# A two-layer float32 transformer kernel on one core: the first transfers regrouped, and four transposes moved behind a projection half

## What is computed

```python
q_a, c_kv, q_idx, k_idx, w_idx, q_b, k_b, v_b = jnp.split(x @ w_in, cuts, axis=-1)
o_a = dsa_attention(q_a, rms_norm(c_kv, kv_norm), q_idx, k_idx, w_idx * IDX_HEADS ** -0.5, w_uk, w_uv)
o_b = stick_breaking_attention(q_b, k_b, v_b)
return concatenate([o_a, o_b]) @ w_out
```

## Time and profile before

| | us |
|---|---|
| median of 3 runs | 619.95 |
| lowest, highest | 619.73, 620.75 |
| the profiled execution | 620.58 |
| its span in the profile | 618.8 |

### The profile page before, as it was taken

The page is one execution under the profiler, slowest core; times in us unless marked ns, Lnnn a source line. Parts: engine busy times, 40 slices in busy tenths (PEclk is TensorE's granted clock), DMA queues, the critical chain, the costliest instruction groups (busy, mean ns, idle before and its releaser), DMA issues.

```text
span 618.8 us, 10403 instructions
## 1 busy us (share of the span) xinstructions
PE 604.3 (98%) x3729; PEld 527.6 (85%) x3729; DVE 413.0 (67%) x668; ACT 340.0 (55%) x631; POOL 25.6 (4%) x49
## 2 busy tenths in 40 slices
PE   7999999999999999999999999999999999999995
PEld 6988887798888888888889998978988888888884
DVE  4698746677756655665887666767776566665546
ACT  5776667266644554455566665653655545555430
POOL 0101012020000000000020000002000000000000
PEclk9999999999999999999999999999999999999999
DMA  7877434447755565555446454362776655555401
GB/s 269 269 222 257 137 103 150 157 135 237 236 174 187 188 203 193 180 184 190 138 145 231 135 164 144 130 211 68 247 235 199 204 201 177 183 187 198 139 1 68
DMA packets 31202, 109.48 MB, mean 177 GB/s; under 512 B 3440, under 2 KB 4464, under 8 KB 31040
## 3 DMA queue, kind: packets, MB, share of 16 engines
q1 hardware_dynamic: 29600, 102.77, 50.2%
q0 software_dynamic: 1568, 6.23, 3.1%
HBM read 107.94 MB, written 1.05 MB: 176 GB/s over the span
## 4 chain that ended last, share of the span: by engine, by line
PE 90%; DMA 3%; DVE 2%; ACT 2%; SPq 1%; POOL 1%; issue 1%; DVEq 0%
PE bank L947 27%; PE bank L879 24%; PE bank L925 13%; PE bank L882 12%; PE bank L893 5%; DMA raw<-stream_in 3%; PE bank L872 2%; PE bank L996 2%; PE bank L1007 1%; PE bank L987 1%; DVE wlo L592 1%; ACT whi L321 1%; POOL hTs L313 1%; PE bank L1194 1%; PE bank L1102 1%
## 5 line engine op out<-in xcount | busy, mean ns | idle before, releaser
L592 DVE TENSOR_TENSOR wlo<-raw,whi 128x1024 fp32r<-128x1024 f32 x190 | 226.6, 1222 | 69.7 <-ACT whi L321 69.5
L321 ACT CAST whi<-raw 128x1024 fp32r<-128x1024 f32 x190 | 192.7, 1049 | 21.1 <-DMA raw<-stream_in 20.8
L879 PE MATMUL bank<-hTs,whi 128*128 128x512 f32 x640 | 160.1, 392 | 0.0
L879 PEld LDWEIGHTS bank<-hTs,whi 128*128 128x128 f32 x640 | 116.1, 189 | 21.4
L947 PE MATMUL bank<-whi,oThi 128*128 128x512 f32 x240 | 94.9, 395 | 0.0
L947 PE MATMUL bank<-whi,oTlo 128*128 128x512 f32 x240 | 93.7, 390 | 0.0
L947 PE MATMUL bank<-wlo,oThi 128*128 128x512 f32 x240 | 93.5, 390 | 0.0
L882 PEld LDWEIGHTS bank<-hTs,wlo 128*128 128x128 f32 x640 | 87.3, 190 | 6.2
L882 PE MATMUL bank<-hTs,wlo 128*128 128x256 f32 x640 | 89.2, 282 | 0.0
L925 PE MATMUL bank<-hTs,whi 128*128 128x256 f32 x320 | 60.3, 288 | 0.0
L947 PEld LDWEIGHTS bank<-whi,oThi 128*128 128x128 f32 x240 | 45.1, 188 | 10.0 <-issue 1.5
(11 more groups left out here) (147 smaller groups left out, 683.3 us busy)
## 6 DMA issues: line engine op xcount, KB each, us to landing
raw<-stream_in SPq DMA_DIRECT2D x190, 512.0 KB, 4.5
qT<-ln_rows_in POOLq DMA_DIRECT2D x8, 512.0 KB, 5.0
v<-xT_in SPq DMA_DIRECT2D x4, 256.0 KB, 4.8
kT<-stream_in SPq DMA_DIRECT2D x4, 256.0 KB, 4.9
h<-x_in POOLq DMA_DIRECT2D x1, 1024.0 KB, 7.4
out<-h SPq DMA_DIRECT2D x4, 256.0 KB, 2.0
dist<-consts_in POOLq DMA_DIRECT2D x1, 384.0 KB, 3.8
ukv<-w_uk_in POOLq DMA_DIRECT2D x1, 256.0 KB, 5.8
```

What stands on the lines that cost most here:

```text
L321: nc.scalar.copy(whi[:, c % RING, j * HW:(j + 1) * HW], raw[:, c % RAW, j * HW:(j + 1) * HW]).then_inc(whi_ready, 1)
L592: nc.vector.tensor_tensor(wlo[:, c % RING, cols], raw[:, c % RAW, cols], whi[:, c % RING, cols].bitcast(F32), ALU.subtract).then_inc(wlo_r ...
L879: mm(dst[:], whi[:, slot, off + k * P:off + (k + 1) * P], hTs[:, k].rearrange("p j s -> p (j s)"), start=(k == 0), stop=False)
```

## The change

Chunk 0 is loaded in four transfers of 512 contiguous floats per partition, so the first two hold the first tile and the last two the second. The order of issue is one of chunk 0, two of xT, one of chunk 0, two of xT, two of chunk 0. ScalarE and VectorE follow this order. TensorE runs 9 warm-up matmuls in place of 11, and then chunk 0 tile by tile: all of the first tile's 24 matmuls, then the second's. The four transposes of w_uk, with their two waits, stand behind the second half of projection 2 in place of before it.

```diff
-        first = kT[:].rearrange("p (j k) s -> p j (k s)", j=2)
-        first_hi_at = whi[:, 0].rearrange("p (j c) -> p j c", j=2)
-        first_lo_at = wlo[:, 0].rearrange("p (j c) -> p j c", j=2)
+        first = kT[:].rearrange("p k s -> p (k s)")
+        FIRST = [slice(i * CW // 4, (i + 1) * CW // 4) for i in range(4)]
...
-        WARM = 11
+        WARM = 9
...
         @block.sync
-            for b in range(4):
-                cols = slice(b * S, (b + 1) * S)
-                sp.dma_start(hT[:, 2 * b:2 * b + 2], xT[:, 2 * b:2 * b + 2]).then_inc(xT_loaded[b], 16)
-                sp.dma_start(first[:, :, cols], stream[0].rearrange("p (j c) -> p j c", j=2)[:, :, cols]
-                             ).then_inc(first_loaded[b], 16)
+            for i in range(4):
+                sp.dma_start(first[:, FIRST[i]], stream[0][:, FIRST[i]]).then_inc(first_loaded[i], 16)
+                if i < 2:
+                    for b in (2 * i, 2 * i + 1):
+                        sp.dma_start(hT[:, 2 * b:2 * b + 2], xT[:, 2 * b:2 * b + 2]).then_inc(xT_loaded[b], 16)
...
         @block.scalar
-            for b in range(4):
-                cols = slice(b * S, (b + 1) * S)
-                act.wait_ge(xT_loaded[b], 16)
-                nc.scalar.copy(hThi[:, 2 * b:2 * b + 2], hT[:, 2 * b:2 * b + 2]).then_inc(hThi_ready, 1)
-                act.wait_ge(first_loaded[b], 16)
-                nc.scalar.copy(first_hi_at[:, :, cols], first[:, :, cols]).then_inc(first_hi, 1)
+            for i in range(4):
+                act.wait_ge(first_loaded[i], 16)
+                nc.scalar.copy(whi[:, 0, FIRST[i]], first[:, FIRST[i]]).then_inc(first_hi, 1)
+                if i < 2:
+                    for b in (2 * i, 2 * i + 1):
+                        act.wait_ge(xT_loaded[b], 16)
+                        nc.scalar.copy(hThi[:, 2 * b:2 * b + 2], hT[:, 2 * b:2 * b + 2]).then_inc(hThi_ready, 1)
...
         @block.tensor
-            for b in range(KT // 2):
-                for j, (w, a) in enumerate(HT_PASSES):
-                    if j == 0:
-                        pe.wait_ge(hThi_ready, b + 1)
-                        pe.wait_ge(first_hi, b + 1)
-                    elif j == 1:
-                        pe.wait_ge(hTlo_ready, b + 1)
-                    else:
-                        pe.wait_ge(first_lo, b + 1)
-                    for k in (2 * b, 2 * b + 1):
-                        for tile in range(2):
+            for tile in range(2):
+                for b in range(KT // 2):
+                    for j, (w, a) in enumerate(HT_PASSES):
+                        if j == 0:
+                            pe.wait_ge(hThi_ready, b + 1)
+                            pe.wait_ge(first_hi, 2 * tile + b // 2 + 1)
+                        elif j == 1:
+                            pe.wait_ge(hTlo_ready, b + 1)
+                        else:
+                            pe.wait_ge(first_lo, 2 * tile + b // 2 + 1)
+                        for k in (2 * b, 2 * b + 1):
                             last = mm(bank[4][:, tile * S:(tile + 1) * S],
...
             for i in range(I_HEADS):
                 dots(i)
+            proj_half(2, 2, 1, False)
             pe.wait_ge(widx_ready, 1)
             pe.wait_ge(par_loaded, 48)
             for j in range(4):
                 last = nc.tensor.transpose(bank[6][:, j * P:(j + 1) * P], ukv[:, 0, j, :], ident)
             last.then_inc(ukT_done, 1)
-            proj_half(2, 2, 1, False)
             proj_half(3, 3, 0, False)
```

More of the change, by code:

```diff
@@ L681, in norm @@
                 split_lo(NORM_CHUNK[n] + AHEAD)
[L684 to L691, removed]
+            for i in range(4):
+                dve.wait_ge(first_hi, i + 1)
+                nc.vector.tensor_tensor(wlo[:, 0, FIRST[i]], first[:, FIRST[i]], whi[:, 0, FIRST[i]].bitcast(F32),
+                                        ALU.subtract).then_inc(first_lo, 1)
+                if i < 2:
+                    for b in (2 * i, 2 * i + 1):
+                        dve.wait_ge(hThi_ready, b + 1)
+                        nc.vector.tensor_tensor(hTlo[:, 2 * b:2 * b + 2], hT[:, 2 * b:2 * b + 2],
+                                                hThi[:, 2 * b:2 * b + 2].bitcast(F32), ALU.subtract
+                                                ).then_inc(hTlo_ready, 1)
             for c in range(1, AHEAD):
@@ L1025, in _ @@
                 mm(bank[j % 4][:], zeros[:, 0:P], zeros[:], start=True, stop=True)
-            for b in range(KT // 2):
-                for j, (w, a) in enumerate(HT_PASSES):
-                    if j == 0:
-                        pe.wait_ge(hThi_ready, b + 1)
-                        pe.wait_ge(first_hi, b + 1)
-                    elif j == 1:
-                        pe.wait_ge(hTlo_ready, b + 1)
-                    else:
-                        pe.wait_ge(first_lo, b + 1)
-                    for k in (2 * b, 2 * b + 1):
-                        for tile in range(2):
+            for tile in range(2):
[9 more added lines that the diff above has]
+                        for k in (2 * b, 2 * b + 1):
                             last = mm(bank[4][:, tile * S:(tile + 1) * S],
                                       w[:, 0, (tile * KT + k) * P:(tile * KT + k + 1) * P], a[:, k, :],
-                                      start=(k == 0 and j == 0 and tile == 0), stop=(k == KT - 1 and j == 2),
-                                      skip_group_check=True)
+                                      start=(k == 0 and j == 0), stop=(k == KT - 1 and j == 2))
             last.then_inc(chunk_used, 1)
```

## The result

| | before | after |
|---|---|---|
| median, us | 620.00 (4 runs) | 623.74 (4 runs) |
| lowest, highest | 619.73, 620.75 | 622.65, 624.17 |
| the profiled execution | 620.58 | 623.36 |
| its span | 618.8 | 621.6 |

The changed kernel takes 1.0056 times as long as before, interval 1.0044 to 1.0069: 3.7 us slower by the medians. I had said 1.2 us slower, with a range up to 622.4; the result lies beyond it. (Each ratio here compares all executions of the two kernels and is not the quotient of the two medians, so the two can differ by a few tenths of a us.)

A forecast was written before the change was run, and what follows sets the result against it. TensorE was taken as the bound, busy 604.3 of 618.8 us, with other engines' chain binding from 27 to 48 us. From the profiled 620.58, -0.3 + 1.5 gave 621.78, or 621.15 against the median; range 619.6 to 622.4.

The forecast's parts named there:

- The moved transposes: Transposes behind projection 2: ScalarE's copy of the turned keys waits, delaying chunk 4's casts and VectorE; 1.5 us slower.
- The transfers: At the start: wider rows of chunk 0 let the ninth transfer land sooner; 0.3 us faster, between 0 and 0.7.
- Chunk 0's matmuls tile by tile, and two warm-up matmuls fewer: TensorE's start: still 48 matmuls, and warm-up ends before the first data are cast; no change in time.
- the cover: Before chunk 1: chunk 0's matmuls end at 14.2 us, ahead of 15.3, so 1.1 us of delay would cost nothing.
- rival 4: At the start: the clock's rise near 6 us is missed, chunk 1 runs at 1.2 GHz; 2.4 us, 623.55; chance 0.07.
- Rivals 1 and 2: First: moved transposes cost nothing, 619.65, chance 0.12. Second: the start gains 1 us, not 0.3, 620.45, chance 0.13.
- Rival 3: Chunk 6's refill, issued 1.5 us later, may land 1 us later still; 622.15; chance 0.12.
- 512 B as the least transfer for line rate: Skill's rule for the start's transfers: wider rows bring 0, and the sum would be 0.3 us higher.

The follow-up runs named there:

- e2: The changed kernel with the transposes back before projection 2's second half, so only the start is changed: 621.79 us against 620.05, ratio 1.0026.
- e1: The kernel before with only the four transposes of w_uk moved behind projection 2's second half: 621.64 us against 620.05, ratio 1.003.
- e3: e1 with ScalarE's copy of the turned keys moved behind chunk 4's casts and projection 2's copy: 620.09 us against 620.05, ratio 1.0004.
- e5: e2 with 11 warm-up matmuls in place of 9: 620.94 us against 620.26, ratio 1.0005.
- e4: e2 with nine matmuls on zeros before the first tile's third pair of k-blocks: 620.15 us against 620.05, ratio 0.9997.
- e9: e3 with VectorE taking chunk 4's differences before the latent's scaling, the fifth top-k round behind slot 0's sums: 620.54 us against 620.17, ratio 1.0007.
- e11: e9 with VectorE taking chunk 5's differences ahead of the first top-k round: 619.55 us against 620.32, ratio 0.9987.
- e7: The kernel before, 1 KB rows kept, with transfers, casts and differences in the changed kernel's order: 619.91 us against 620.26, ratio 0.9995.
- e10: e2 with the queue waiting for the first transfer to land before issuing the fifth: 619.9 us against 620.32, ratio 1.0.
- e12: The changed kernel with e10's pacing, seven matmuls on zeros in the hole, and the orders of e11: 619.48 us against 620.14, ratio 0.9986.
- e6: e2 with transfers, casts and differences alternating xT and chunk 0 as before, 2 KB rows kept: 621.9 us against 620.26, ratio 1.003.

## Why the prediction was wrong, step by step

The step that failed is the start: I priced the regrouped transfers at 0.3 us of gain, and the tile order with the shorter warm-up at nothing, and by e2 they cost 1.7 us together.

- *The moved transposes, 1.5 us slower*: right in place, sign and size. e1 gives 1.6, e3 shows that it is ScalarE's order, and the two waits of TensorE stand where they were forecast: in the changed kernel, 2.0 us before the stick scores (I had said 1 to 1.5) and 0.7 before `stick_rest` (0.8). The wait of 0.4 before the transposes went, and nothing came of it.
- *The transfers, 0.3 us faster*: this is the term that failed, in sign too. I had asked only how fast 2.1 MB move and when the ninth transfer lands. It came as before, cast from 13.14 against 13.21; over all traces from 12.89 to 13.62 with 2 KB and no pause, and 12.62 to 13.68 with 1 KB, so a gain of 0.3 can't be told from none. What I passed over is when those in between land. I took their landings from the kernel before, position by position, and "an issue holds the queue for 590 ns" was carried over to a queue that no longer alternates between two shapes; it took 432. The fifth was cast 1.8 us later in the changed kernel and 1.5 in e2.
- *"Chunk 0's matmuls tile by tile, and two warm-up matmuls fewer: nothing, under the same cover"*: the cover was 1.1 us, and I had held it against a late last transfer alone. I had also said that the warm-up ends before the first data are cast in either case. With 11 it doesn't: the first two casts are done at 5.50 (4.88 + 0.62), and TensorE takes them up at 6.24, behind the warm-up. With 9 it took them up at 5.54, so it had used up its 12 matmuls sooner and stood longer; e5 leaves open how much that costs. With the fifth late, 36 of 48 matmuls were left at 10.57 us. At the full clock that is 36 x 0.12 = 4.3 us, to 14.9, still in time; in e4, with its last waits for data, chunk 0 ended at 15.45 and chunk 1 began at 15.37. At half the clock for 3.4 us it is not in time: 16.68.
- *The clock, rival 4, 0.07*: its mechanism is what happened, at another place. I feared a rise that is missed at 6 us; the clock rose (the four matmuls at 7.12 took 0.64 us) and fell again behind a hole of 2.6 us. The price, up to 2.4 us, held as a bound for the 1.7. That this rival's sum, 623.55, lies so near the measured 623.74 is luck: it had priced another stretch at the low clock. The chance was too low, because I took the holes of 1.4 and 1.23 us of the kernel before, which cost no clock, as proof for longer ones. From the Trainium skill, TensorE: Matmul & The Clock Gate, section What's actually happening, I had quoted that activity releases the throttle. That agrees with e4, where matmuls on zeros in the hole keep the granted clock at 1.00 and end the loss.
- *Rivals 1 and 2* (no cost from the transposes, a larger gain at the start) are out by e1 and e2. *Rival 3*, that the refill of chunk 6 takes longer than before: 5.84 us in place of 5.41 in the changed kernel's profile, 0.4 of the 1 us I had priced.
- *512 B as the least transfer for line rate* (the Trainium skill, DMA: Bandwidth & Descriptors, section Specifications): by that rule the wider rows bring nothing, and the ninth, within 0.1 us of before, agrees; its scatter over the traces is too wide to rule my 0.3 out.

With a start at no cost, the sum would have been 620 + 1.5 = 621.5; with the measured 1.7 it is 623.2, against 623.74. In the changed kernel's profile chunk 4's differences come 2.38 us later than before and the refill behind them takes 0.43 longer, which makes the 2.8 us of the span.

## What to carry to other kernels

Before a step is moved on one engine, look at which engine takes its result and what stands behind that on its queue: here a copy of 0.6 us, waiting 1.8 us (e1), delayed casts, a buffer's refill and the scores behind them, and moving that copy back on its engine cured it. A stage that is done a microsecond early isn't free to be rearranged: ask how much work is at hand at each arrival, and whether TensorE would stand for longer than it ever did in the trace, since the price then can be the clock and not the hole. When a gain shows only once the next two waits are moved along with it (e9, e11), follow the chain one link at a time.

## What the runs showed of the hardware that I hadn't expected

- The queue's issue time depends on what it issued before: transfers of xT with 2 KB rows took 0.59 us (median) between ones with two rows of 1 KB, and 0.43 us among their own kind. In e7, where they come in pairs between rows of 1 KB, the first of a pair took 0.57 and 0.60 us, and the shortest of the four 0.42.
- Faster issue made the middle transfers land later: the fifth of eight, issued at 2.7 us, at 9.88, and in e10, issued at 4.05, it was cast at 8.76; in e12, with the same pause, at 9.04. The ninth, too, came 0.9 us sooner with the pause (12.01 in e10, against 12.89 in e2). Why the memory side is slower with more under way, no run here shows.
- The clock fell to one half during or right behind holes of 2.6, 1.9, 2.6 and 1.7 us (changed kernel, e2, e5, e10), and about 2 us behind one of 2.3 in e6, but not behind holes of 1.4 and 1.23 us in the kernel before nor one of 1.81 in e3. Neither the length of the hole nor the busy share around it sorts these cases: e3 kept its clock behind a longer hole than e10's, and with TensorE busy for 2.97 of the 5 us from 10 to 15. What decides, no run here shows. How long the clock stayed low differed too: 3.4 us in the changed kernel, about 6.8 in e2.
